# Gating and output projection of the even layer as one pipeline, with the scale-and-offset of both normalisations on ScalarE

## What is computed

```python
# B: chunked spatial gating on ub, vb, gb, three column blocks of h (512 wide each)
vn = layer_norm(v, ln_g, ln_b)                        # over 512 channels
mixed = einsum('gij,bcjgd->bcigd', tril(w_s), vn) + b_s   # 8 groups x 64 channels, 128x128 per group
ob = (u * mixed) * silu(gb)                           # silu(gb) and silu(ga) are already stored in h
# output projection of the even layer
out = concatenate([oa, ob], axis=-1) @ e_w_out        # 1024 x 1024
x = layer_norm(ALPHA * x + out, ln_g[0], ln_b[0])     # over 1024 channels
```

## Time and profile before

| | us |
|---|---|
| median of 3 runs (2318.27 to 2323.5) | 2320.27 |
| the profiled execution | 2321.72 |
| its span, first to last instruction | 2319.7 |
| gating, from its first issue to that of `eo` | 876.98 to 978.63 |
| `eo`, to the first issue of the next phase | 978.63 to 1145.01 |

### The profile page before, as it was taken

The page is one execution under the profiler, slowest core; times in us unless marked ns, Lnnn a source line. Parts: engine busy times, 40 slices in busy tenths (PEclk is TensorE's granted clock), DMA queues, the critical chain, the costliest instruction groups (busy, mean ns, idle before and its releaser), DMA issues. The chain is left out here.

```text
span 2319.7 us, 36604 instructions
## 1 busy us (share of the span) xinstructions
PE 1866.1 (80%) x14710; PEld 1116.0 (48%) x14710; DVE 1215.4 (52%) x2174; ACT 537.9 (23%) x1080; POOL 397.2 (17%) x370
## 2 busy tenths in 40 slices
PE   8998649899948993779658999959899567663888
PEld 4445225444416773734324666634545357662433
DVE  2000076888897666424476677675532223232485
ACT  0000016300115540000055555551212012221000
POOL 0001110000024551100000333310032202213110
PEclk9999779999978995589878999979898787887899
DMA  4200822223111006150244354454772564543610
GB/s 170 73 32 31 228 81 84 91 73 109 37 55 48 19 15 222 67 218 37 76 107 149 122 153 142 134 132 72 146 176 70 161 171 97 148 112 84 238 64 38
DMA packets 301606, 248.30 MB, mean 107 GB/s; under 512 B 158764, under 2 KB 252236, under 8 KB 301180
## 3 DMA queue, kind: packets, MB, share of 16 engines
q1 hardware_dynamic: 294516, 224.36, 33.3%
q10 hardware_dynamic: 3952, 12.65, 1.5%
q0 software_dynamic: 2976, 9.02, 1.1%
HBM read 162.78 MB, written 87.71 MB: 108 GB/s over the span
## 5 line engine op out<-in xcount | busy, mean ns | idle before, releaser
L1610 PE MATMUL ri_ps<-ri_xm,ri_w 128*128 128x384 f32 (+1 forms) x768 | 231.3, 455 | 0.3 <-ACT ri_big L1739 0.3
L555 PE MATMUL ix_ps<-ix_src,ei_xT 128*128 128x512 f32 x512 | 222.3, 596 | 8.3 <-DMA ix_src<-in_e_w_in 8.3
L1706 PE MATMUL ri_ps<-ri_w,ri_xm 128*128 128x512 f32 x512 | 226.8, 606 | 0.0
L186 PE MATMUL ei_ps<-ei_w,ei_xT 128*128 128x512 f32 (+1 forms) x432 | 189.1, 600 | 4.0 <-DMA ei_w<-in_e_w_in 4.0
L1610 PEld LDWEIGHTS ri_ps<-ri_xm,ri_w 128*128 128x128 f32 x768 | 144.2, 190 | 72.8 <-issue 0.7
L633 DVE TENSOR_SCALAR_CACHE_REDUCE ix_flags<-score,ix_cand 128x384 bf16<-128x384 f32 (+1 forms) x186 | 163.7, 943 | 12.2 <-DVE ix_cand L650 12.0
L555 PEld LDWEIGHTS ix_ps<-ix_src,ei_xT 128*128 128x128 f32 x512 | 97.6, 191 | 130.6 <-issue 122.0
L1706 PEld LDWEIGHTS ri_ps<-ri_w,ri_xm 128*128 128x128 f32 x512 | 99.4, 195 | 124.5 <-issue 124.4
L1185 PE MATMUL co_psm<-co_w,co_srcT 128*128 128x512 f32 (+1 forms) x288 | 130.1, 611 | 11.2 <-DVE co_y L1240 10.4
L186 PEld LDWEIGHTS ei_ps<-ei_w,ei_xT 128*128 128x128 f32 (+1 forms) x432 | 77.9, 181 | 114.4 <-issue 114.4
L1185 PE MATMUL eo_psm<-eo_w,eo_srcT 128*128 128x512 f32 (+1 forms) x288 | 125.6, 594 | 0.0
(11 more groups left out here) (337 smaller groups left out, 3025.5 us busy)
## 6 DMA issues: line engine op xcount, KB each, us to landing
ix_src<-in_e_w_in SPq DMA_DIRECT2D x4, 2048.0 KB
scratch_h<-ix_stage SPq DMA_DIRECT2D x32, 256.0 KB
ri_w<-in_c_w_in SPq DMA_DIRECT2D x16, 512.0 KB, 5.7
ri_w<-in_c_w_in SPq DMA_DIRECT2D x4, 2048.0 KB, 8.5
ei_w<-in_e_w_in SPq DMA_DIRECT2D x3, 2048.0 KB
scratch_h<-ei_stage POOLq DMA_DIRECT2D x24, 256.0 KB, 2.3
ix_src<-scratch_h SPq DMA_DIRECT2D x3, 2048.0 KB, 12.0
gt_uvg<-scratch_h SPq DMA_DIRECT2D x8, 768.0 KB, 10.8
```

Source lines behind the costliest of these rows:

```text
L186: last = nc.tensor.matmul(ps[n % NB][0:rows(t), 0:cw], xT[:, kd, t * P:t * P + rows(t)], rhs, start=(kd == 0), stop=(kd == KD - 1))
L555: last = nc.tensor.matmul(ps[n % NB][:], xT[:, kd, t * P:(t + 1) * P], w_rest[s % 2][:, kd], start=(kd == 0), stop=(kd == KD - 1))
L1610: last = nc.tensor.matmul(out[:, 0:wd], w[:, ct % 2, kd, i * P:(i + 1) * P], xm[:, i, kd, lo:lo + wd], start=(kd == 0), stop=(kd == KD - 1))
L1706: last = nc.tensor.matmul(out[:], xm[:, j, kd, t * P:(t + 1) * P], w[:, a, kd], start=(kd == 0), stop=(kd == KD - 1))
```

## The change

One phase, `phase_gate_out`, takes the place of both. It runs 12 steps, and in step s the gating of tile s, the transposes of tile s-1, the projection of tile s-2 and the closing normalisation of tile s-3 are issued. The gated half of a tile is written by VectorE straight into the source tile in SBUF; only the attention half is loaded from `cat` (now 512 columns wide, without the sample rows). The source, residual and `uvg` tiles have rings of three buffers in place of nine each, so that later loads wait for earlier tiles. In both normalisations VectorE computes an offset of one column, minus mean times rstd, and ScalarE does `scale * x + offset` with per-row operands. SP's queue issues everything. The last two of the six loads counted by `c_in` come behind the two weight halves. The sample logits come behind the gating of tile 0, and the other sample steps move accordingly. The scratch `cat` shrinks; the other phases are as they were.

```diff
-def phase_gating(nc, g, beside):
+def phase_gate_out(nc, g, score_s, lrow, x_of):
...
+            sp.dma_start(ident[:], g["c_ident"]).then_inc(id_in, 16)
+            sp.dma_start(ws[:], g["b_ws"].rearrange("g i j -> i g j")).then_inc(id_in, 16)
+            load_uvg(0)
+            sp.dma_start(upper[:], g["c_uppereq"]).then_inc(c_in, 16)
+            sp.dma_start(bgam[:], g["b_ln_g"].partition_broadcast(P)).then_inc(c_in, 16)
+            sp.dma_start(bbet[:], g["b_ln_b"].partition_broadcast(P)).then_inc(c_in, 16)
+            sp.dma_start(bs[:], g["b_bs"].rearrange("g i -> i g"), **small).then_inc(c_in, 16)
+            load_src(0)
+            load_uvg(1)
+            load_w(0)
+            load_w(1)
+            sp.dma_start(w00[:], ...).then_inc(c_in, 16)
+            sp.dma_start(b00[:], ...).then_inc(c_in, 16)
             side.loads(sp)
+            load_src(1)
+            load_res(0)
+            sp.dma_start(gam[:], g["ln_g"][0].partition_broadcast(P)).then_inc(g_in, 16)
+            sp.dma_start(bet[:], g["ln_b"][0].partition_broadcast(P)).then_inc(g_in, 16)
+            load_uvg(2)
+            load_src(2)
+            load_res(1)
+            side.pages(sp)
+            load_res(2)
+            for s in range(1, NT + 4):
+                if s + 2 <= LAST:
+                    load_uvg(s + 2)
...
+                if s >= 4:
+                    store(s - 4)
+                    if s - 1 <= LAST:
+                        load_res(s - 1)
+                if s + 2 <= LAST:
+                    load_src(s + 2)
...
         @block.tensor
+            def mixed(t):
+                pe.wait_ge(vn_d, t + 1)
+                if t:
+                    pe.wait_ge(gated, t)
+                for h in range(H): ...            # 8 matmuls of 64 columns
+            def transposes(t):
+                pe.wait_ge(gated, t + 1)
...
+            def project(t):
+                pe.wait_ge(srcT_d, 2 * t + 2)
+                if t >= 2:
+                    pe.wait_ge(y_d, t - 1)
...
+            pe.wait_ge(id_in, 32)
+            for gg in range(2): ...               # transposes of the mixing weights
+            pe.wait_ge(wsT_d, 2)
+            for s in range(NT + 3):
+                if s < NT:
+                    mixed(s)
+                if s == 3:
+                    side.turn(pe)
+                if 4 <= s < 4 + DB // 2:
+                    side.values(pe, 2 * (s - 4))
+                if s == NT:
+                    pe.wait_ge(gated, NT)
+                    side.turn_back(pe)
+                if 1 <= s <= LAST + 1:
+                    transposes(s - 1)
+                if s >= 2:
+                    project(s - 2)
         @block.scalar
+            for s in range(NT + 4):
+                if s <= LAST:
+                    act.wait_ge(boff_d, s + 1)
+                    if s >= 2:
+                        act.wait_ge(mix, s - 1)
+                    nc.scalar.activation(vn[0:m, k], slot(uvg, s)[:, AW:2 * AW], ACT.Identity, scale=brs[0:m, k:k + 1], bias=boff[0:m, k:k + 1]).then_inc(bnorm_d, 1)
+                if s == 2:
+                    side.scalar(act)
+                if 1 <= s <= LAST + 1: ...        # two copies of the transposed tile s-1; each waits for tr
+                if s >= 3:
+                    act.wait_ge(off_d, t + 1)
+                    nc.scalar.activation(y[0:m, k], y[0:m, k], ACT.Identity, scale=rstd[0:m, k:k + 1], bias=off[0:m, k:k + 1]).then_inc(norm_d, 1)
         @block.vector
+            def normalise(t):                     # bn_stats, bn_aggr, + eps, then
+                dve.wait_ge(brstd_d, t + 1)
+                nc.vector.scalar_tensor_tensor(boff[0:m, k:k + 1], bmv[0:m, k, 0:1], -1.0, brs[0:m, k:k + 1], ALU.mult, ALU.mult).then_inc(boff_d, 1)
+                dve.wait_ge(bnorm_d, t + 1)
...                                               # gain, bias; vn_d
+            def gate(t): ...                      # waits sg_d, mix; bias, product into src[:, AW:D]; gated
+            def finish(t): ...                    # waits mm, res_in; as L1233 to L1240, L1238 replaced as above
+            dve.wait_ge(c_in, 16 * 6)
+            for gg in range(2): ...               # masks the mixing weights
+            for s in range(NT + 4):
+                if s <= LAST:
+                    normalise(s)
+                if s == NT:
+                    side.by_channel(dve)
+                if 1 <= s <= LAST + 1:
+                    gate(s - 1)
+                if s == 1:
+                    side.logits(dve)
+                if s == 2:
+                    side.shares(dve)
+                if s == 4:
+                    side.own_value(dve)
+                if s == LAST + 1:
+                    side.gate(dve, src[0:DB, LAST % RING, 0:AW])
+                if s >= 3:
+                    finish(s - 3)
...
 def dsa_gmlp_rwkv7_step(nc, g):
-    even_layer(nc, g)
...
-    phase_out(nc, "eo", g["c_ident"], g["cat"], g["e_w_out"], x_of, g["ln_g"][0], g["ln_b"][0],
-              lambda t: [((0, rows(t)), tile(g["x1"], t))], Nothing)
+    even_layer(nc, g, lambda t: tile(g["x_prompt"], t) if t < NT else g["x_sample"])
```

More of the change, by code:

```diff
@@ new lines, in by_channel, with gate @@
+    def by_channel(self, dve):
+        dve.wait_ge(self.pv, DB // 2)
+        pso = self.ps_v.rearrange("p (b c j) -> p c b j", b=DB, c=4)
+        for j in range(2):
+            r = j * HD
+            ins = self.nc.vector.tensor_copy(self.oT[r:r + HD, :, :], pso[r:r + HD, :, :, j])
+        ins.then_inc(self.oT_d, 1)
+    def gate(self, dve, out):
+        dve.wait_ge(self.back, 1)
+        self.link(self.nc.vector.tensor_tensor(out, self.ps_o[0:DB, :], self.vp[:], ALU.add))
+        self.nc.vector.tensor_tensor(out, out, self.ga[:], ALU.mult).then_inc(self.done, 1)
@@ new lines, in turn, with values @@
+    def turn(self, pe):
+        pe.wait_ge(self.probs, 1)
+        for pg in range(2):
+            for h in range(H):
+                k = (pg * H + h) * DB
+                last = self.nc.tensor.transpose(self.ps_p[:, k:k + DB], self.lrow[:, h, pg * P:(pg + 1) * P], self.ident[0:DB, 0:DB])
+        last.then_inc(self.tr, 1)
+    def values(self, pe, b0):
+        pe.wait_ge(self.pT_d, 1)
+        pe.wait_ge(self.cache_in, 16 * 2 * DB)
+        for b in range(b0, b0 + 2):
+            for ct in range(4):
+                for pg in range(2):
+                    k = (b * 4 + ct) * 2
+                    last = self.nc.tensor.matmul(self.ps_v[:, k:k + 2], self.vc[:, b, pg, ct * P:(ct + 1) * P], self.pT[:, pg, 2 * ct:2 * ct + 2, b],
+                                                 start=(pg == 0), stop=(pg == 1))
+        last.then_inc(self.pv, 1)
@@ L1012, in _ @@
+            store(LAST)
             sp.wait_ge(stored[0], 16 * 5)
@@ L1076, in _ @@
-        @block.tensor
-        def _(pe):
-            pe.wait_ge(c_in, 16 * 8)
+                for half in range(2):
+                    cs = slice(half * AW, (half + 1) * AW)
+                    link(nc.vector.scalar_tensor_tensor(y[0:m, k, cs], slot(res, t)[:, cs], ALPHA, ps_m[k][0:m, cs], ALU.mult, ALU.add))
+                    link(nc.vector.bn_stats(st[0:m, half], y[0:m, k, cs]))
+                link(nc.vector.bn_aggr(mv[0:m], st[0:m].rearrange("p a b -> p (a b)")))
+                nc.vector.tensor_scalar(veps[0:m, k:k + 1], mv[0:m, 1:2], LN_EPS, None, ALU.add).then_inc(var_d, 1)
@@ L1079, in _ @@
             for gg in range(2):
+                dve.wait_ge(ws_tr, gg + 1)
                 for j in range(4):
[L1081 to L1092 removed]
@@ L1241, in _ @@
                 dve.wait_ge(y_d, t + 1)
-class Nothing:
-    late = ()
-    def __init__(self, *buffers):
-        pass
-    def loads(self, sp):
-        pass
-    def sync(self, eng, t):
-        pass
-    tensor = scalar = gpsimd = vector = sync
 JR, JW, JK, JV, JA, JG = range(6)
```

385 lines of the change are left out of this document (204 added, 181 removed).

## The result

| | us | runs |
|---|---|---|
| before | 2320.57 (2318.27 to 2323.5) | 4 |
| after | 2288.42 (2281.19 to 2289.42) | 4 |
| ratio | 0.9854, 95% interval 0.9831 to 0.9877 | |
| forecast | 2281, range 2266 to 2302 | |

The kernel is 32.2 us faster; 39.7 were forecast. The median lies in the stated range and 0.4 us above the range of 2275 to 2288 that the forecast had given as its own. The profiled execution took 2289.42 (span 2287.6, clock 0.884). Its changed stretch begins with the issue of `go_ident` at 880.39 and ends with the first issue of the next phase at 1116.98: 236.6 us in place of 268.0, so 31.4 of the 32.3 us between the two profiled executions lie in it.

What follows compares the result with a forecast made beforehand. Gating was taken as bound by VectorE's chain, then half-clock TensorE; projection by a load, then full-clock TensorE. Joining gains 47.7 us, less 8 for the clock: 39.7, giving 2281 us, range 2266 to 2302.

Steps and rivals of the forecast that it cites:

- rival 2: Steps with values: clock falls at each block's head and returns late, costing 25 us; 2298 us, chance 0.15.
- 876.98 + 22.5, about 900: Start: VectorE waits for loads behind 7.2 MB, 18 us, plus 2.5 until data flows and 2 to land.
- rival 3: Start: the two small loads are not held up by the weights, 14 us earlier; 2267 us, chance 0.06.
- The first normalisation, 4.5 us: Gating: 4.77 before; ScalarE's pass 0.83 plus 0.35 for small operation and hand-over; bounds 4.2 and 5.8.
- The 3.4 for a block of values: TensorE's values at full clock: half of 6.79 us, as the 64-column block halves; bounds 6.79 and 3.4.
- I take 8: Clock loss in four steps with values: 2.0 us each from wide matmuls at half clock; bounds nothing and 25 us.
- rival 1: Steps with values: the clock stays at 2.4 GHz, gain 47.7 us; 2273 us, chance 0.20.
- it waits 3.1 us: ScalarE's queue: closing pass stands behind copies until 7.2 us into a step with values; VectorE ready at some 4.1.
- Rival 4: Hand-overs between VectorE, ScalarE and GpSimd exceed their slack, 2 us in seven steps, 14 us; 2295 us, chance 0.08.
- 9.96 + 0.7: Tail: 9.96 us before, plus 0.7 for ScalarE's 1024-wide pass, a small operation and two hand-overs.
- Rival 5: Merged pipeline's wide matmuls run at 1.2 GHz, 13.74 us more per tile; 2396 us, chance 0.04.
- rival 6: The stages do not overlap, as VectorE's order makes each wait for the other; no change, 2320 us, chance 0.02.

Runs made afterwards that it cites:

- r2: The changed kernel with the small constant loads and sample-row loads issued ahead of the weights: 2275.31 us, 0.9808 of the kernel before.
- r9: The changed kernel with small loads first, values in pieces, normalising passes on VectorE and GpSimd's product behind VectorE's pass: 2264.39 us, 0.9752 of before.
- r7: The changed kernel with GpSimd's product issued behind VectorE's offset operation: 2284.06 us, 0.9842 of the kernel before.
- r5: The changed kernel with the sample values left out, one small matmul in place of 16 per block: 2263.26 us, 0.9758 of the kernel before.
- r6: The changed kernel with each step's values cut into four pieces between the projection's wide matmuls: 2276.04 us, 0.9807 of the kernel before.
- r8: The changed kernel with logits and all sample steps one step later, values in three blocks instead of four: 2284.39 us, 0.983 of before.
- r3: The changed kernel with both normalising passes back on VectorE: 2282.67 us, 0.9847 of the kernel before.
- r11: The changed kernel with gain and bias of the closing normalisation left out: 2283.79 us, 0.9836 of the kernel before.
- r10: r9 with the logits and other sample steps one step later: 2256.71 us, 0.9727 of the kernel before.
- r12: r10 with the third tile's gating inputs and the second source tile's attention half loaded ahead of the output weights: 2260.02 us, 0.9741 of before.
- r4: The kernel before, two phases kept, with both normalising passes put on ScalarE: 2322.44 us, 1.0007 of the kernel before.

## Why the prediction was right

The order of events was as forecast and the time lies in the range. The miss in the stretch is 8.3 us (236.6 against 268.0 - 39.7 = 228.3): 3.1 up to the first wide matmul, 3.6 for the clock (11.6 against 8), and 1.6 over the first projection, the rest of TensorE's work and the tail. All three have the same sign: the time is not right through errors that cancel. The result lies between the forecast and rival 2.

1. **VectorE's first operation, "876.98 + 22.5, about 900".** Measured phase +24.3, with 23.0 taken: 1.3 late. No row was given for the two terms beside the bytes, 2.5 and 2 us. That the loads ahead in the queue hold it was right: r2 took them away and won 14.1 us, where rival 3 had said 14. But it was not only their bytes in flight: SP came to issue the last of the two small loads at phase +13.4 in place of +4.5 (it stood 3.7 us at the weights and 4.5 us at the next load), which is 9.0 of the 14.2 us by which VectorE starts later than in r2.
2. **The first normalisation, 4.5 us.** 5.28 was measured (906.30 to 911.58), inside the stated bounds of 4.2 to 5.8. The bound's own condition came true: the small operation is held up by GpSimd's product. It was in the trace of before, since L1051 took 1.48 us for what takes 0.55 ahead of the product (r9). Three normalisations make 2.3 us, and the two terms with 0.5 won elsewhere give the first wide matmul at phase +58.7 against +55.6. The Trainium skill ("SBUF — State Buffer", SBUF: two separate sides) has a rule for it: VectorE and GpSimd share a port pair that the one who starts first holds for its whole instruction against, among others, a VectorE operation with two inputs in SBUF. The traces agree: 0.160 us alone, 1.213 beside the product; in r7 the gain, issued while the product runs, ends 0.55 us behind it; and in r9 a product of 1.77 in place of 1.27 where the gain started first. The bound of 5.8 would have been the better choice of the two ends.
3. **Steps.** 16.45 was forecast without values, 16.57 measured (r5); 19.85 with values at full clock, 19.92 measured (r6). The 3.4 for a block of values, taken for half of 6.79, was right: 3.35 by these two runs, in pieces (3.5 with the small matmul that r5 keeps). No run shows an unbroken block at the full clock to its end.
4. **The clock, "I take 8".** This is the term that was mis-sized most: 22.8 - 19.92 = 2.9 us a step, 11.6 in all by r6 and by r5. The fall came in the middle of the block, not late in it, and the clock stayed at 0.50 to about 981.7 (the windows of its fall above): the rest of the values (some 3 us), all of the transposes and about 2 us of projection ran at half speed (in the third step half as much), where the prediction had priced only wide matmuls. With larger blocks (r8, 7.3 and 8.3 us of values) steps of 25.0 and 26.6 came of it. Against it stood rival 1 (nothing; refuted by the windows, true only of r6's order) and rival 2 (25 us; half of that). The Trainium skill ("TensorE: Matmul & The Clock Gate", What's actually happening) ties the clock to how busy the engine has been. In these windows the clock is at 0.50 while instructions keep the engine 1.00 busy, so the reading of that sentence on which rival 1 stood does not hold here.
5. **ScalarE's queue, "it waits 3.1 us".** VectorE waits up to 6.1 us for L1154 (975.67 to 981.80). The pass itself and its hand-over are 1.3 of these, as in the tail; the other 4.8 are the queue, against 3.1 in the forecast, because the copies ahead of it wait for transposes at half clock (done at 9.3 us after the start of the step, forecast 7.2). It still costs nothing: TensorE waits for none of it. r3 and r11 show that VectorE's work is behind TensorE's. Rival 4 is refuted for the kernel as it stands, and r8 shows where it would begin.
6. **The tail, 9.96 + 0.7.** 10.75 measured.
7. **Rival 5 (slower, wide matmuls at 1.2 GHz)** falls by the windows at 1.00, **rival 6** by the time and by the start of mixing inside each step. What was not foreseen is how much of the start belongs to the order of loads in SP's queue beyond the two constants (r10, r12).

What share of the 32 us each part brought is shown as far as r3 and r4 go: the joining all of it, the ScalarE pass none that can be measured. Inside the joining no run separates the parts (no barrier and reload between the phases, loads in the shadow of work, mixing and values mostly at the full clock); the traces show their sum, the first wide matmul at phase +58.7 in place of +127.6.

## What to carry to other kernels

When two stages are joined, the order of loads in one queue is part of the change: put what the first operation waits for ahead of large weights, and when one load is moved up ask which is the next to be late. In a kernel like this one, thin matmuls in small pieces between wide ones kept the clock that a block of them lost. Moving work off an engine that is not the bound won nothing here, and beside a GpSimd product an operation of one column can cost as much as the product.

## What the runs showed of the hardware

- The same 32 thin matmuls (2 columns, 128x128 weights) cost 3.35 us in four pieces of 8 between wide ones at a clock of 1.00 (r6 against r5); pieces of 16, 1.84 us long, kept 1.00 too (r10). In one block behind the mixing, the clock fell to 0.50 for some 6.7 us in three of four steps and for 3.4 in the other, at 2.9 us a step in the mean.
- A VectorE operation on 128x1 takes 0.16 us alone and 1.21 beside a GpSimd product of 1.26. Behind a later product the hold passes to the next operation (0.69 to 1.01 in r7, 0.69 to 1.64 in r9), and in r9 the sum did not change.
- ScalarE's pass with both operands per row took 0.814 us for 512 columns and 1.242 for 1024; 0.83 and 1.26 had been estimated.
- Small loads behind 4 MB of weights in the same queue delayed the start by 14 us, 9.0 of them through their later issue (r2 against the change).
